# A PEER decoder block on one core: gate banks evicted ahead of the weight rounding, a reordered gate stage, a search over 136 pair sums and a moved projection rounding

## The reference, cut to what matters

```python
q = (xt @ wq).reshape(t, PEER_HEADS, 2, PEER_HALF_DIM)          # 8 heads, two halves
sc = jnp.einsum('thpc,hpnc->thpn', q, sub_keys)                 # 128 keys for each half
top_v, top_i = lax.top_k(sc, PEER_TOPK)                         # 16 of each half
cand_v = (top_v[:, :, 0, :, None] + top_v[:, :, 1, None, :]).reshape(t, PEER_HEADS, kk)   # 256 pair sums
best_v, best_pos = lax.top_k(cand_v, PEER_TOPK)                 # the best 16 pairs
...
hc = jnp.einsum('cd,chkd->chk', xc, u[ec])                      # 128 experts of 16384 per token
ac = gc * jax.nn.gelu(hc)
return jnp.einsum('chk,chkd->cd', ac, v[ec])
```

## Time and profile before

| | |
|---|---|
| median of 3 runs | 3025.43 us |
| their range | 3022.53 to 3033.47 us |
| time of the profiled execution | 3030.26 us |
| its span, first to last instruction | 3028.2 us |
| TensorE busy | 2958.6 us (98%) |
| VectorE busy | 2483.1 us (82%) |
| ScalarE busy | 1056.5 us (35%) |
| GpSimd busy | 803.8 us (27%) |
| mean granted TensorE clock | 0.990 |

### The profile page before, as it was taken

One profiled execution on the slowest core, in us unless ns is written; L12 is line 12 of the kernel. 1 busy time (PEld: TensorE's weight loads), 2 busy tenths in 40 slices (PEclk: granted clock), 3 DMA queues, 4 the chain that ended last, 5 costly groups with the idle time before them and its releaser, 6 DMA issues.

```text
span 3028.2 us, 45428 instructions
## 1 busy us (share of the span) xinstructions
PE 2958.6 (98%) x17342; PEld 2756.6 (91%) x17342; DVE 2483.1 (82%) x3616; ACT 1056.5 (35%) x1429; POOL 803.8 (27%) x535
## 2 busy tenths in 40 slices
PE   9999999999998989999999999999999999999997
PEld 7777778899888989999999999999999999999786
DVE  7544444489998869999999999999999999998644
ACT  5224432222234653323333333333333333334422
POOL 0120000037666102222222222233333333332100
PEclk9999999999999999999999999999999999999998
DMA  4243122335457679999999999999999999994222
GB/s 172 87 156 111 70 84 97 111 108 119 113 119 238 241 264 356 365 357 380 360 373 377 365 382 368 369 377 367 370 372 377 360 376 366 370 366 171 91 97 97
DMA packets 206883, 779.61 MB, mean 257 GB/s; under 512 B 50512, under 2 KB 100176, under 8 KB 132432
## 3 DMA queue, kind: packets, MB, share of 16 engines
q1 hardware_dynamic: 134176, 414.03, 37.7%
q0 software_dynamic: 67680, 358.71, 32.6%
q10 hardware_dynamic: 4944, 5.81, 0.5%
HBM read 745.35 MB, written 33.10 MB: 257 GB/s over the span
## 4 chain that ended last, share of the span: by engine, by line
PE 68%; DVE 18%; DMA 6%; issue 3%; SPq 3%; POOL 1%; ACT 1%; DVEq 0%; ACTq 0%; POOLq 0%
PE bank L630 21%; PE bank L631 20%; PE bank L632 20%; DVE row L1923 4%; DVE w_lo L1567 4%; SPq L585 2%; DMA raw_b_whole<-in_u_t 2%; DMA raw_whole<-in_u_t 2%; DVE h L2104 1%; PE bank L721 1%; POOL gate_matrix L2307 1%; DVE w_lo L1554 1%; PE bank L924 1%; PE bank L744 1%; PE bank L722 1%
## 5 line engine op out<-in xcount | busy, mean ns | idle before, releaser
L630 PE MATMUL bank<-x_hi,w_hi 128*128 128x342 f32 (+1 forms) x2880 | 1001.3, 348 | 31.7 <-DVE w_lo L1567 16.7
L631 PE MATMUL bank<-x_lo,w_hi 128*128 128x342 f32 (+1 forms) x2880 | 996.4, 346 | 0.0
L632 PE MATMUL bank<-x_hi,w_lo 128*128 128x342 f32 (+1 forms) x2880 | 989.8, 344 | 0.0
L630 PE MATMUL bank<-a_hi,w_hi 128*128 128x342 f32 x2048 | 652.8, 319 | 3.9 <-DVE w_lo L1554 2.5
L632 PE MATMUL bank<-a_hi,w_lo 128*128 128x342 f32 x2048 | 652.7, 319 | 0.0
L631 PE MATMUL bank<-a_lo,w_hi 128*128 128x342 f32 x2048 | 650.3, 318 | 0.0
L630 PEld LDWEIGHTS bank<-x_hi,w_hi 128*128 128x128 f32 x2880 | 547.2, 190 | 77.2 <-DVE w_lo L1567 19.2
L631 PEld LDWEIGHTS bank<-x_lo,w_hi 128*128 128x128 f32 x2880 | 546.1, 190 | 38.2 <-issue 1.2
L632 PEld LDWEIGHTS bank<-x_hi,w_lo 128*128 128x128 f32 x2880 | 545.9, 190 | 38.2
L630 PEld LDWEIGHTS bank<-a_hi,w_hi 128*128 128x128 f32 x2048 | 387.4, 189 | 6.5 <-issue 3.0
L631 PEld LDWEIGHTS bank<-a_lo,w_hi 128*128 128x128 f32 x2048 | 387.5, 189 | 0.0
(11 more groups left out here) (258 smaller groups left out, 3227.3 us busy)
## 6 DMA issues: line engine op xcount, KB each, us to landing
raw_whole<-in_v_t SPq DMA_DIRECT2D x62, 1024.0 KB, 7.9
raw_b_whole<-in_v_t SPq DMA_DIRECT2D x62, 1024.0 KB, 7.6
raw_b_whole<-in_u_t SPq DMA_DIRECT2D x46, 1024.0 KB, 9.4
raw_whole<-in_u_t SPq DMA_DIRECT2D x46, 1024.0 KB, 9.0
raw_whole<-in_u_t SPq DMA_DIRECT2D x72, 512.0 KB, 3.4
beside<-gate_matrix SPq DMA_DIRECT2D x32, 704.0 KB, 15.0
raw_whole<-in_w_o SPq DMA_DIRECT2D x32, 512.0 KB, 3.5
raw_whole<-in_w_q SPq DMA_DIRECT2D x32, 512.0 KB, 3.4
```

Source lines behind the costliest of these rows:

```text
L630: pe.matmul(out, w_hi[slot][:, blk, :], m_hi, start=first, stop=False)
L631: pe.matmul(out, w_hi[slot][:, blk, :], m_lo, start=False, stop=False)
L632: return pe.matmul(out, w_lo[slot][:, blk, :], m_hi, start=False, stop=last)
```

## The change

- The pair search covers 136 sums: the 8 best of half one with all 16 of half two, and ranks 8 to 15 of half one with rank 0 of half two. The positions are turned back into two ranks with one more instruction (`low_over`), and one CAST becomes two TENSOR_TENSORs.
- In the gate stage ACT evicts a set's banks before it rounds either half of the next unit. On DVE U_ALONE+8's halves stand around row dot 2, ahead of the second one-hot set; row dots 3, 4, 5 move from ahead of the loop, set 3 and set 13 to sets 1, 7 and 15. POOL gathers row 1 two ranks after row 0.
- The first group's gates: SP loads 9 of 11 token blocks ahead of the last store and of U_PEER+3; ACT copies the other two from the blocks still in SBUF; DVE waits for these copies too. The preparation of rows for tokens 342 to 383 moves behind the third chain of the group on ACT, and behind the first v unit on PE.
- In the projection ACT rounds U_PROJ+1 after chunk 11 instead of 15, DVE after chunk 8 instead of 11.

```diff
 TOPK = 16
+FULL = TOPK // 2
+PAIRS_ALL = FULL * TOPK + TOPK - FULL
 NK = 128
...
         carrier = at("carrier", one + 54 * K, [P, 1])
-        cand = at("cand", one + 18 * K, [P, TC, TOPK, TOPK])
-        cand_cut = at("cand_cut", one + 22 * K, [P, TC, TOPK * TOPK])
+        cand = at("cand", one + 18 * K, [P, TC, PAIRS_ALL])
+        cand_cut = at("cand_cut", one + 22 * K, [P, TC, PAIRS_ALL])
+        low_over = at("low_over", one + 51 * K + 512, [P, TC * TOPK], U32)
         pick = [at(f"pick{i}", one + (26 + 2 * i) * K, [P, TC * TOPK, TOPK], BF16) for i in range(2)]
...
         g_first = sem("g_first")
+        g_copied = sem("g_copied")
         g_stored = [sem(f"g_stored{i}") for i in range(2)]
...
 
-        PER_TOPK = 23
+        PER_TOPK = 24
         ROPE_STEPS = 11
...
                 load_alone(PLAIN + i)
+            for s in range(2):
+                sp.wait_ge(g_stored[s], 16 * (ONE_TB // 2 - s))
+            sp.wait_ge(gates_put, 16 * TOPK * PH)
+            sp.wait_ge(spill_stored, 16)
+            sp.wait_ge(weights_used, U_PEER + 1)
+            sp.dma_start(g_tile[0][:, 0:N_TB - 2, :, :],
+                         g_dram[0:N_TB - 2, :, 0:GROUP, :].rearrange("b j i t -> j b i t")).then_inc(g_in[0], 16)
+            sp.dma_start(h_pre[0][:, :, :], by_quarters(h_dram[0])).then_inc(h_in[0], 16)
             for b in range(stored, ONE_TB):
...
             load_unit(U_PEER + 3, packed(u_t, GROUP))
-            for s in range(2):
-                sp.wait_ge(g_stored[s], 16 * (ONE_TB // 2))
+            sp.dma_start(g_dram[N_TB - 1, :, TOPK:NK, :], g_blk[(ONE_TB - 1) % 2][:, TOPK:NK, :]).then_inc(g_stored[0], 16)
+            sp.wait_ge(g_stored[1], 16 * (ONE_TB // 2))
             sp.wait_ge(g_first, 16)
-            sp.wait_ge(gates_put, 16 * TOPK * PH)
             sp.wait_ge(spill_stored, 16 * N_GROUPS)
...
 
-            sp.wait_ge(weights_used, U_PEER + 1)
-            load_g(0, 0)
-            sp.dma_start(g_dram[N_TB - 1, :, TOPK:NK, :], g_blk[(ONE_TB - 1) % 2][:, TOPK:NK, :]).then_inc(g_stored[0], 16)
             peer_group(0, 0, first=True)
...
                                   scaled=None if first and k == 0 else scaled)
-                    if first and k != 1:
-                        sparse_rows_b(k)
-                        sparse_rows_b(k + 1)
+                    if first and k == 0:
+                        sparse_rows_b(0)
+                        sparse_rows_b(1)
                     if last:
...
                         second_product(g, par, q, u, slot, first, keeping, ends)
+                    if first and q == 0:
+                        sparse_rows_b(2)
+                        sparse_rows_b(3)
 
...
                 b, e = divmod(q, TB // OH)
-                for i in range(GATE_UNITS):
-                    if begun(i) == q:
-                        hi_half(PLAIN + i + 1, 0)
                 if e == 0:
...
                     if begun(i) == q:
+                        hi_half(PLAIN + i + 1, 0)
                         hi_half(PLAIN + i + 1, 1)
...
 
+            act.wait_ge(g_out, (TB // OH) * 2 * ONE_TB)
+            act.wait_ge(weights_used, U_PEER + 1)
+            for b in range(ONE_TB - 2, ONE_TB):
+                act.activation(g_tile[0][:, b + PUT_TB, :, :], g_blk[b % 2][:, 0:GROUP, :], ACT.Copy).then_inc(g_copied, 1)
 
...
                     gated_hi(0, a_slot(0, par))
-                    activate(p, a_slot(3, par))
-                    hi_peer(g, 2, par, first=True)
+                    gelu(p)
+                    hi_peer(g, 2, par, halves=(0,), first=True)
+                    gated_hi(p, a_slot(3, par))
+                    hi_peer(g, 2, par, halves=(1,), first=True)
                     activate(p + 1, a_slot(1, par))
...
                     between(2, p + 1, a_slot(1, par))
-                if first:
-                    rows_evict_b(0)
-                    rows_evict_b(1)
-                    rows_stage_b(2)
-                    rows_stage_b(3)
                 if last:
...
                     between(3, p + 2, a_slot(2, par))
+                    if first:
+                        rows_evict_b(0)
+                        rows_evict_b(1)
+                        rows_stage_b(2)
+                        rows_stage_b(3)
                     between(4, p + 3, a_slot(0, 1 - par))
...
                             third_hi(c)
+                            if c == 11:
+                                hi(U_PROJ + 1, (U_PROJ + 1) % 2, ahead=N_AHEAD)
 
...
 
-            hi(U_PROJ + 1, (U_PROJ + 1) % 2, ahead=N_AHEAD)
             for n in range(0, DC, 2):
...
 
-                step(dve.tensor_tensor(cand[:, :, :, :],
-                                       t_v[0][:, :, :].unsqueeze(3).to_broadcast([P, TC, TOPK, TOPK]),
-                                       t_v[1][:, :, :].unsqueeze(2).to_broadcast([P, TC, TOPK, TOPK]), ALU.add),
+                runs = [P, TC, FULL, TOPK]
+                dve.tensor_tensor(cand[:, :, FULL * TOPK:PAIRS_ALL], t_v[0][:, :, FULL:TOPK],
+                                  t_v[1][:, :, 0:1].to_broadcast([P, TC, TOPK - FULL]), ALU.add)
+                step(dve.tensor_tensor(cand[:, :, 0:FULL * TOPK].rearrange("p t (a b) -> p t a b", b=TOPK),
+                                       t_v[0][:, :, 0:FULL].unsqueeze(3).to_broadcast(runs),
+                                       t_v[1][:, :, :].unsqueeze(2).to_broadcast(runs), ALU.add),
                      max_next=True)
-                top16(step, b_v, b_pos, cand[:, :, :, :].rearrange("p t a b -> p t (a b)"), cand_cut, TOPK * TOPK, **more)
+                top16(step, b_v, b_pos, cand, cand_cut, PAIRS_ALL, **more)
 
...
                 step(dve.tensor_scalar(pos_hl[:, 1, :], flat, 15, None, ALU.bitwise_and))
-                step(dve.tensor_copy(pos_b[:, :, :, :], pos_hl[:, :, :].unsqueeze(3).to_broadcast([P, 2, TC * TOPK, RUN])))
+                step(dve.scalar_tensor_tensor(low_over[:, :], flat, float(FULL * TOPK), pos_hl[:, 1, :], ALU.is_ge, ALU.mult))
+
+                def in_runs(tile):
+                    return tile.unsqueeze(2).to_broadcast([P, TC * TOPK, RUN])
+
+                dve.tensor_tensor(pos_b[:, 0, :, :], in_runs(pos_hl[:, 0, :]), in_runs(low_over[:, :]), ALU.add)
+                step(dve.tensor_tensor(pos_b[:, 1, :, :], in_runs(pos_hl[:, 1, :]), in_runs(low_over[:, :]), ALU.subtract))
                 runs = [P, TC * TOPK, TOPK // RUN, RUN]
...
             lo(U_ALONE + 7, (U_ALONE + 7) % 2, halves=(1,))
+            lo(U_ALONE + 8, U_ALONE % 2, halves=(0,))
             row_dot(2, 0, row_loads(2))
+            lo(U_ALONE + 8, U_ALONE % 2, halves=(1,))
             one_hots(1, 1)
-            lo(U_ALONE + 8, U_ALONE % 2)
-            row_dot(3, 1, row_loads(3))
             for q in range(N_OH):
...
                             lo_half_of(PLAIN + i + 1, half)
-                for k, at_set in ((4, 3), (5, 13), (6, N_OH - 2), (7, N_OH - 1)):
+                for k, at_set in ((3, 1), (4, 7), (5, 15), (6, N_OH - 2), (7, N_OH - 1)):
                     if at_set == q:
...
                 dve.wait_ge(g_in[par], 16 * n + 16)
+                if isinstance(j, int) and j <= GROUP:
+                    dve.wait_ge(g_copied, 2)
                 dve.tensor_tensor(h_a[:, :, :], h_g[:, :, :], g_tile[par][:, :, m, :], ALU.mult).then_inc(e_gated, 1)
...
                     proj_out(c - 8)
-                if c == 11:
+                if c == 8:
                     lo(U_PROJ + 1, (U_PROJ + 1) % 2)
...
                         load_row(0)
+                    if hd == PH - 2 and k == TOPK // 2 + 2:
                         load_row(1)
...
```

## The result

The changed kernel takes 3008.65 us, median of five runs (3003.24 to 3015.15), against 3029.1 us for the kernel before in five runs beside it (3022.53 to 3033.47). The ratio is 0.9942, with a 95% interval of 0.9922 to 0.9962: faster by 0.6%. The forecast was 3003.5, the range 2994 to 3014. Seven more executions of the same kernel in another job (3005.63 to 3019.43) have a median of 3011.62, ratio 0.9954 (0.9938 to 0.9970). Over all jobs the median of 36 executions of the kernel before is 3026.1 and that of 12 of the changed one 3010.3: 16 us (20 in the first job alone), where the forecast's sum was 22.

What follows compares the result with a forecast made beforehand. TensorE, busy for 2958.6 of 3028.2 us, bounds the kernel; only its idle and slow-clock time can be won. Terms 1.9 + 4.5 + 5.2 + 5 + 5.6 = 22 us, from the median 3025.43 to 3003.5; range 2994 to 3014.

Steps and rivals of the forecast that it cites:

- The search: Last head's pair search: fewer sums shorten VectorE's work, and PE gains 1.9 us, between nothing and 3.8.
- in heads 1 to 7 I cost it at nothing: Heads 1 to 7: the shorter search gains nothing, since PE does not wait for VectorE there.
- U_ALONE+8 and dot 2: Low parts around row dot 2: the 5.21 us wait and 1.5 of clock go, 2.2 come back; net 4.5 us.
- the sign of being right: Signs listed beforehand, among them no PE wait over 1 us for U_ALONE+8, a gate bank or U_PEER+3.
- The row itself comes no earlier: Row for dot 2: GpSimd's chain starts from head 7, whose end does not move, so dot 2 begins near 941.
- Eviction first: Gate stage: banks come free at once, so the 3.49 us wait and 1.7 of clock go; gain 5.2 us.
- The first group's gates: First group: gates load 7 to 8 us sooner, VectorE's gate moves to about 1088.3; gain 5 us.
- the first rival: Loads hold first group and projection: the 5.13 us wait becomes a longer one a unit later; gain 14.2, 3011 us; chance 0.12.
- The projection: Low parts of U_PROJ+1 sooner: 3.98 us of wait and 2.9 of clock go, 1.3 come back; gain 5.6 us.
- The third rival: Projection's copy blocked by GpSimd's adds on the shared port: this part gains 3.4 or 0.5, 3008.6 us at worst; chance 0.05.
- DVE holding the gate stage: Rival, gate stage: eviction's gain goes into one-hot waits, row dots' places cost 2 us; gain 14.8, 3010.6 us; chance 0.10.
- the slower case: Rival, gate stage: rounding late in each of eleven units costs 23 us, eviction's 5.2 not won; 3031.6 us; chance 0.07.

Runs made afterwards that it cites:

- e1: The kernel before with only the search over 136 sums; one run, 3025.2 us.
- e5: The kernel before again, without an edit; one run, 3023.16 us.
- e6: The kernel before with only the first group's gates loaded early, the two copies on ScalarE and that group's new order; one run, 3023.16 us.
- e9: The kernel before with only the eviction ahead of the rounding in the gate stage; one run, 3023.61 us.
- e3: The changed kernel again, without an edit; seven runs, 3011.62 us, ratio 0.9954.
- e4: The changed kernel with the copy of product 1 ahead of U_PROJ+1's low parts, copies 3, 5, 7 one place sooner; six runs, 3006.46 us, ratio 0.9934.
- e7: The kernel of e4 with the first group's third GELU and gate ahead of rounding the first v unit; six runs, 3009.07 us, ratio 0.9935.
- e8: The kernel of e4 with the spilled scores' load behind the next group's first u unit load; six runs, 3008.32 us, ratio 0.9938.
- e10: The kernel of e4 loading half of each expert row in the peer stage, leaving out half the rows' data; four runs, 2982.17 us, ratio 0.9852.
- e2: The kernel before with only U_ALONE+8's halves around row dot 2, the row dots' new places and row 1 loaded later; one run, 3030.64 us.

## Why the prediction was right, and where not

The time came out 5 us above the forecast (3008.65 for 3003.5), inside the range. The sum of 22 was too large by about 6, and its terms err in both directions, so part of the nearness is luck. I set the mean of the traces that have a part against the mean of those that don't, the two of before among them.

**The search:** 1.9 forecast, 4.0 found by 940 us (-3.6 in seven traces with it, +0.4 in five without). The price per instruction was right: FIND_INDEX8 over 136 elements takes 292 ns, where it took 416 over 256.

```profile
L1818 DVE FIND_INDEX8 b_pos<-b_v,cand 128x8 uint32<-128x136 f32 x8 | 2.3, 292 | 0.0
```

What failed is the sentence "in heads 1 to 7 I cost it at nothing". It holds for heads 1 to 6. At the end of head 7 PE waits for VectorE, and 2.1 us are won by 880 us. Whether what is won by 940 is kept depends on the next part: e1 shows that with the old order the wait behind row dot 2 takes nearly all of it back. So the two parts belong together. From 800 to 1000 us the six traces with both gain 8.1 us on average, four with neither (before, e5, e6, e9) 1.3: 6.8 for the two, where 1.9 and 4.5 make 6.4. Alone they gain 2.8 (search) and 3.3 (order), that is 1.5 and 2.0 more than those four, which scatter by 5 among themselves; 3.5 together at most. So the forecast's two terms come out near in their sum, but not as two gains that add, and that much is luck.

**U_ALONE+8 and dot 2:** 4.5 forecast, 3.0 found between 940 and 1000 us (-4.3 in seven traces, -1.2 in five without). The mechanism is right: the wait is gone and short ones came, though not all as short as the sign of being right asked (none over 1 us for a gate bank): 2.02 us in e3 and 2.77 in e4. The size was read from one trace, whose row took 9.0 us from issue to use; where it takes 5.6, there is only 1.94 us of wait to remove. What failed besides is "The row itself comes no earlier". With both parts GpSimd issues it at 929.2 to 931.4 (six traces), where each part alone leaves it at 932.2 and 932.7, and dot 2 begins at 936.7 to 939.0 and not near 941. The check built on that, that VectorE cannot end the stage before about 1066, is broken too: the matmul that started at 1078.08 starts at 1063.8 to 1064.3 in four of the six (after, e7, e8, e10).

**Eviction first:** 5.2 forecast, 5.2 in every trace that has it. In the four traces with both old orders (before, e5, e1, e6) this wait is 3.49, 3.60, 2.96 and 3.37 us. But e2 shows that the new order alone removes it too: at this place the two parts are two ways to win the same 5 us, which the prediction didn't see. It costed the row dots' new places at nothing, and there the step failed. GpSimd and ScalarE in before, where dot 5 stands at set 13, and in e2, where it stands at set 15:

```profile
1011.94 1.74 POOL L2326 DMA_INDIRECT early_row<-in_u_rows,expert  x1 [37.68 <-DVE early_row L1923]
```

```profile
1019.82 1.74 POOL L2326 DMA_INDIRECT early_row<-in_u_rows,expert  x1 [31.65 <-DVE early_row L1923]
```

```profile
1016.42 1.06 ACT L1106 ACTIVATE w_hi<-raw_whole 128x1024 fp32r<-128x1024 f32 x1 [2.82 <-DMA raw_whole<-in_u_t]
```

The end of dot 5 frees a buffer and GpSimd loads the next row into it. In before this load goes out 4 us ahead of the half of a unit that ScalarE rounds next (issued at 1015.90), and that half lands after 7.3 us; the DMA engines are at 0.93 from 1012 to 1020. In e2 the half is issued first, at 1013.16, and lands after 3.2 us; the DMA engines are at 0.44 in the 8 us around it. In e1, e5, e6 and e9 the row load is again 4 us ahead, and the half takes 6.8 to 7.5 us. So the wait of 3.49 was made by a row load in front of a weight load, and either moving the dot or evicting first removes it; no run has the dot's move by itself. Between 940 and 1040 the order alone gives 8.4 us (one trace). The eviction alone gives 8.9, of which 3.7 fell to it before its place, with a wait of only 1.16 for U_ALONE+8. Both together give 9.4 on average, in after, e3, e4, e7 and e8.

**The first group's gates:** 5 forecast, 3.0 found (-3.9 in the five traces with it and full rows but not e7, -0.9 in five without). VectorE's gate was put at 1088.3, which is 1074.1 with the 14.2 us won before it; the trace has it at 1073.96, and no wait for its load:

```profile
1073.96 0.53 DVE L2040 TENSOR_TENSOR beside<-beside 128x352 f32<-128x352 f32 x1 [2.06 <-ACT beside L1436]
```

What came next was the load of the first v unit, issued at 1080.10, with ScalarE waiting 5.68 us for it:

```profile
1087.79 1.06 ACT L1117 ACTIVATE w_hi<-raw_whole 128x1024 fp32r<-128x1024 f32 x1 [5.68 <-DMA raw_whole<-in_v_t]
```

This is the first rival's mechanism, and the prediction's own sign for it, a wait of over 4 us for the first v unit, is there. Its price was too high: it took all 5 us away, and 3 remain, because the wait of 2.47 us for the second v unit shrinks to 0.89.

**The projection:** 5.6 forecast, 3.0 found (-3.4 in two traces, -0.4 in six without). The step that failed is "a low part of weights between 1.15 and 1.9": beside GpSimd's sums it takes 2.28 us, and 1.22 alone. The copy behind was then wanted 2.55 us too soon instead of 1.3, and a wait of that length lost clock again (1.5 us: 0.17 of 9.0). The third rival had this mechanism, with a gain of 3.4 or 0.5. The Trainium skill's rule for it (SBUF — State Buffer, "Who interferes with whom": the loser of the shared port is blocked for the whole of the other's instruction) is borne out in kind. By its length a low part behind a whole add could take 3.1 us, an estimate (1.22 and an add of 1.87 us in after); it takes 2.28.

**The middle:** nothing was forecast. Over its 1625 us the six traces with the code of before (the first among them) lie between -4.1 and 9.9, the five of the changed kernel and its variants between -0.9 and 6.3; their means, 1.6 and 3.0, differ by less than either group scatters. That arriving early is paid back is thus not shown, nor excluded to 1 or 2 us. With it the terms found add up: 4.0 + 3.0 + 5.2 + 3.0 + 3.0 = 18.2, less 1.4 is 16.8, beside 16 us in the medians of all executions.

What PE waits for there is the DMA, by e10. The prediction saw the 0.97 and named VectorE beside it; a share of 0.97 at 371 GB/s was the bound. A figure of the Trainium skill would have spoken against that: Perfetto Trace Analysis, "Roofline", gives about 435 GB/s as the ceiling of one core's 16 DMA engines, of which 371 are 85%. The runs do not bear it out as a test for this load, more than half of whose DMA time goes to GpSimd's row loads (queue and kind, packets, MB, share of the 16 engines' span; 1250 to 1730 us of after); the busy share was the better sign.

```profile
q0 software_dynamic: 14428, 105.09, 57.5%
q1 hardware_dynamic: 24624, 71.34, 39.5%
```

DVE holding the gate stage, and the slower case, are excluded by the 5.2 us kept in all traces. ScalarE's roundings do come later (VectorE waits 4.6 us for them in after), and PE has its low parts in time all the same.

**The version that is best:** e4, the changed kernel with the copy first, 5.4 to 5.6 us instead of 2.7 to 4.1 in its stretch in each of four kernels that have it. In the times of whole executions this does not stand clear of the changed kernel: the intervals overlap. e7 and e8 add nothing that can be measured.

## What to carry to other kernels

Before a wait is priced, ask how it was made, back to the transfer if there is one. The wait behind row dot 2 was 5.21, 5.42, 5.08, 1.94 and 1.16 us in five traces with the same order there, by when a row landed and when VectorE came to it: take a second trace before such a wait is priced. The wait of the projection, which only engines and their queues make, was 3.94 to 3.98 us in six. The one for a gate bank hung on a load too, and yet came again each time (2.96 to 3.60 us), since the same row load met it each time; such a wait goes when the order of the two loads changes. Ask of each moved instruction which buffer it frees, and what load starts then. When an instruction is taken from in front of a wait, put what the critical engine asks for first at the head of the queue, ahead of what is merely slow. And where the DMA engines are busy for 0.97 of a stage, be ready for what e8 and e10 show here: another order of loads moved the waits about, and fewer bytes removed them.

## What the runs showed of the hardware that was not expected

Executions of one kernel, and of kernels with the same code up to there, agree to half a microsecond over the first 800 us, and differ by up to 5.7 us in what they take from 940 to 1000 us, the place where GpSimd scatters gates and loads rows at the same time. A load of 512 KB (half of a unit) landed 3.2 us behind its issue in e2 and 6.8 to 7.5 us in the five traces where a row load had gone out 4 us before it. A VectorE TENSOR_TENSOR with two inputs in SBUF, 1.22 us alone, took 2.28 beside GpSimd's TENSOR_TENSOR in one kernel and 1.97 in e4.
